# Two transformer blocks on one core: copies of short rows, compressed turns, column sums and the first weight unit rearranged

## What is computed

```python
def first_block(x, ...):
    h = rms_norm(x, attn_pre_norm)
    mix = hybrid_mixer(h, ...)            # differential attention (4 heads) and sparse attention (8 heads)
    x = x + rms_norm(mix, attn_post_norm)
    h = rms_norm(x, ffn_pre_norm)
    return x + rms_norm((silu(h @ w_gate) * (h @ w_up)) @ w_down, ffn_post_norm)

# in hybrid_mixer: proj = h @ w_in gives dq, dk, dv, nq, kc, vc, ks, vs, kw, vw, gates
# differential: a = softmax(q1 k1) - lam * softmax(q2 k2), causal;  o = a @ v;  rms_norm per head
# sparse: o = g0 * o_cmp + g1 * o_slc + g2 * o_win  (compressed tokens, selected blocks, window)
```

## Time and profile before

| | |
|---|---|
| median of 3 runs | 1940.08 us (1939.52 to 1940.37) |
| the profiled execution | 1938.64 us, its span 1936.7 us |
| TensorE matmul | 1889.7 us busy, 98% |
| TensorE weight load | 1525.7 us, 79% |
| VectorE | 823.8 us, 43% |
| ScalarE | 427.4 us, 22% |
| GpSimd | 1231.2 us, 64% |

### The profile page before, as it was taken

The page is one execution under the profiler, slowest core; times in us unless marked ns, Lnnn a source line. Parts: engine busy times, 40 slices in busy tenths (PEclk is TensorE's granted clock), DMA queues, the critical chain, the costliest instruction groups (busy, mean ns, idle before and its releaser), DMA issues.

```text
span 1936.7 us, 25810 instructions
## 1 busy us (share of the span) xinstructions
PE 1889.7 (98%) x9462; PEld 1525.7 (79%) x9462; DVE 823.8 (43%) x1419; ACT 427.4 (22%) x868; POOL 1231.2 (64%) x737
## 2 busy tenths in 40 slices
PE   9999989999999999999999999999999999999997
PEld 7876558888888888866888888889877888888886
DVE  6345872633432025424453434104993464334103
ACT  4333651311110012015221111002333331111000
POOL 7973544866666558654786667656757586666662
PEclk9999999999999999999999999999999999999998
DMA  6431002233333224330233333221323222333311
GB/s 205 132 119 44 1 2 72 76 92 97 90 111 105 90 62 141 88 98 2 76 98 97 91 93 123 93 81 52 109 76 98 77 84 90 97 93 111 105 60 44
DMA packets 44879, 168.30 MB, mean 87 GB/s; under 512 B 4984, under 2 KB 7288, under 8 KB 44672
## 3 DMA queue, kind: packets, MB, share of 16 engines
q1 hardware_dynamic: 44064, 162.99, 27.5%
q10 hardware_dynamic: 736, 4.21, 0.5%
HBM read 165.07 MB, written 2.11 MB: 86 GB/s over the span
## 4 chain that ended last, share of the span: by engine, by line
PE 81%; DVE 6%; POOL 3%; issue 2%; ACT 1%; POOLq 0%; DVEq 0%; ACTq 0%
PE psum L496 25%; PE psum L498 25%; PE psum L497 25%; POOL w_lo L408 1%; DVE h_lo L1351 1%; PE psum L676 1%; DVE tmp L1393 1%; PE psum L690 1%; PE psum L541 1%; DVE e_ring L1508 1%; POOL w_hi L405 1%; POOL x L419 1%; PE psum L717 0%; PE psum L549 0%; PE psum L763 0%
## 5 line engine op out<-in xcount | busy, mean ns | idle before, releaser
L408 POOL TENSOR_TENSOR w_lo<-raw,w_hi 128x1024 fp32r<-128x1024 f32 (+1 forms) x287 | 753.0, 2624 | 23.9
L496 PE MATMUL psum<-h_hi,w_hi 128*128 128x512 f32 (+1 forms) x1816 | 689.8, 380 | 10.8 <-POOL w_lo L408 6.8
L497 PE MATMUL psum<-h_lo,w_hi 128*128 128x512 f32 (+1 forms) x1816 | 685.4, 377 | 0.0
L498 PE MATMUL psum<-h_hi,w_lo 128*128 128x512 f32 (+1 forms) x1816 | 685.3, 377 | 0.0
L405 POOL TENSOR_SCALAR w_hi<-raw 128x1024 fp32r<-128x1024 f32 (+1 forms) x287 | 325.0, 1132 | 514.0 <-PE psum L498 484.0
L496 PEld LDWEIGHTS psum<-h_hi,w_hi 128*128 128x128 f32 x1816 | 342.1, 188 | 83.3 <-issue 10.3
L498 PEld LDWEIGHTS psum<-h_hi,w_lo 128*128 128x128 f32 x1816 | 341.9, 188 | 70.3
L497 PEld LDWEIGHTS psum<-h_lo,w_hi 128*128 128x128 f32 x1816 | 341.9, 188 | 69.3 <-issue 0.2
L496 PE MATMUL psum<-g_hi,w_hi 128*128 128x512 f32 (+1 forms) x594 | 219.9, 370 | 0.0
L497 PE MATMUL psum<-g_lo,w_hi 128*128 128x512 f32 (+1 forms) x594 | 219.4, 369 | 0.0
L498 PE MATMUL psum<-g_hi,w_lo 128*128 128x512 f32 (+1 forms) x594 | 219.3, 369 | 0.0
(11 more groups left out here) (261 smaller groups left out, 1797.5 us busy)
## 6 DMA issues: line engine op xcount, KB each, us to landing
raw<-in_wide SPq DMA_DIRECT2D x239, 512.0 KB, 3.6
raw<-in_down SPq DMA_DIRECT2D x48, 704.0 KB, 4.0
x<-in_xt ACTq DMA_DIRECT2D x4, 512.0 KB, 6.8
decay<-decay_rows ACTq DMA_DIRECT2D x1, 2048.0 KB, 7.5
out<-x SPq DMA_DIRECT2D x16, 128.0 KB, 1.7
o_diff<-in_angles SPq DMA_DIRECT2D x1, 512.0 KB, 6.8
cols<-in_cols SPq DMA_DIRECT2D x1, 221.0 KB, 4.0
tabs<-in_tables SPq DMA_DIRECT2D x1, 208.0 KB, 6.0
```

The source lines that it names most:

```text
L408: nc.gpsimd.tensor_tensor(w_lo[:, slot, 0:w], raw[:, j % RAW, 0:w], w_hi[:, slot, 0:w].bitcast(F32), ALU.subtract).then_inc(units_split, 1)
L496: pe.matmul(out_ap, lhs[0], rhs[0], start=first, stop=False)
L497: pe.matmul(out_ap, lhs[0], rhs[1], start=False, stop=False)
L498: return pe.matmul(out_ap, lhs[1], rhs[0], start=False, stop=last)
```

## The change

Five edits. (1) Copies of the transposed maps: ScalarE makes one in every step, and in sparse steps with i of 0 or 1 it copies both banks; VectorE only bank 5 of sparse steps with i of 2 or 3. The one-instruction combination stays on VectorE for i = 3 alone; i = 2 goes to GpSimd as a product and a sum. (2) `cmp_turn` 1 and 2 with their scores stand behind dv1 and dv2. (3) The last square of an opening norm goes to PSUM, VectorE adds it to `total` too, and `col_stat` makes one column sum; it stands behind chunk 2 of the fourth unit, `row_stat` behind chunk 5. (4) Opening: unit 0 is split in halves (`split_first`); SyncE loads x's last three quarters right behind unit 0 and no longer waits; TensorE takes the first four chunks of kc when the first half is split, and from the fourth on alternates chunks of kc and vc, three apart; the column sum stands behind vg0 and the row behind vg1. (5) ScalarE loads its first table ahead of x, and takes lambda's exponential ahead of the squares.

```diff
-BOTH_BY_DVE = (0, 1)
+COPIED_BY_ACT = (0, 1)
 def combined_by_dve(t):
-    return STEPS[t][0] == "diff" and STEPS[t][3] >= 2
+    return STEPS[t][0] == "diff" and STEPS[t][3] == NB - 1
 def copies_by_dve(upto):
-    return sum(step[0] == "nsa" or step[3] in BOTH_BY_DVE for step in STEPS[:upto])
+    return sum(step[0] == "nsa" and step[3] not in COPIED_BY_ACT for step in STEPS[:upto])
...
                 for j in range(peel):
-                    if j == 1:
-                        sp.wait_ge(x_landed[2], 16)
                     load(tiles, source, j, j)
+                    for q in range(1, 4 if j == 0 else 0):
+                        sp.dma_start(x[:, 2 * q:2 * q + 2, :], xt[:, 2 * q:2 * q + 2, :]).then_inc(x_landed[q], 16)
...
+            def split_first(tiles):
+                w = tiles * P
+                pool.wait_ge(weights_landed[0], n.take("landed_0", 16))
+                pool.sem_inc(unit_taken, 1)
+                for part, high_done, low_done in ((slice(0, w // 2), first_high, first_half), (slice(w // 2, w), high_split, units_split)):
+                    nc.gpsimd.tensor_scalar(w_hi[:, 0, part], raw[:, 0, part], 1.0, 1.0, ALU.mult, ALU.mult).then_inc(high_done, 1)
+                    pool.wait_ge(high_done, 1)
+                    nc.gpsimd.tensor_tensor(w_lo[:, 0, part], raw[:, 0, part], w_hi[:, 0, part].bitcast(F32), ALU.subtract).then_inc(low_done, 1)
+                n.take("units")
...
             def col_stat():
-                pe.wait_ge(summed, n.take("summed", SUMS))
-                add_columns(total, True, False)
-                pe.wait_ge(squared, n.take("squared", KC))
-                add_columns(squares[:, (KC - 1) % 2, :], False, True)
+                n.take("squared", KC)
+                pe.wait_ge(summed, n.take("summed", KC - 1))
+                add_columns(total, True, True)
...
-                    if t == 0:
+                    if t == 2:
                         col_stat()
-                    if t == 3:
+                    if t == 5:
                         row_stat()
...
-            feature("kc", 0)
-            feature("vc")
-            pe.wait_ge(summed, n.take("summed", KC - 1))
-            n.take("squared", KC)
-            add_columns(total, True, True)
+            n.take("units_split", 2)
+            for t in range(KC + 3):
+                for u, c in ((0, t), (1, t - 3)):
+                    if not 0 <= c < KC:
+                        continue
+                    if u == 0:
+                        pe.wait_ge(h_low, c + 1)
+                    if c in (0, KC // 2):
+                        pe.wait_ge(units_split if u or c else first_half, u + 1)
+                    mm = three(psum[:, u, :], [w_hi[:, u, c * P:(c + 1) * P], w_lo[:, u, c * P:(c + 1) * P]], h_of(c), c == 0, c == KC - 1)
+                    if c == KC - 1:
+                        mm.then_inc(unit_done, 1)
             pe.wait_ge(lam_exped, 1)
-            for u in token_units("vg", (3, 3, 2), VG, row_stat):
-                pass
+            for u in token_units("vg", (3, 3, 2), VG):
+                if u == 0:
+                    col_stat()
+                if u == 1:
+                    row_stat()
...
             for u in token_units("dv", (2, 2, 2, 2), 4 * P):
-                if u in (0, 1):
-                    cmp_turn(u + 1)
-                    cmp_scores(u + 2)
+                if u in (1, 2):
+                    cmp_turn(u)
+                    cmp_scores(u + 1)
...
-                place = total[:] if j == 0 else squares[:, 1, :] if j == KC - 1 else psum[:, 4 + j % 2, :]
+                place = psum[:, 4 + j % 2, :] if j else total[:]
...
-                    if 0 <= r < len(STEPS) and STEPS[r][3] not in BOTH_BY_DVE:
+                    if 0 <= r < len(STEPS):
...
-                        copy(t_ring[:, r % 2, 0, 0:w], psum[:, 4 + (r % 2 if STEPS[r][0] == "diff" else 0), 0:w]).then_inc(pair_copied_act, 1)
+                        if STEPS[r][0] == "nsa" and STEPS[r][3] in COPIED_BY_ACT:
+                            copy(t_ring[:, r % 2, :, 0:w], psum[:, 4:6, 0:w]).then_inc(pair_copied_act, 1)
+                        else:
+                            copy(t_ring[:, r % 2, 0, 0:w], psum[:, 4 + (r % 2 if STEPS[r][0] == "diff" else 0), 0:w]).then_inc(pair_copied_act, 1)
...
-            for j in range(4):
-                act.dma_start(x[:, 2 * j:2 * j + 2, :], xt[:, 2 * j:2 * j + 2, :]).then_inc(x_landed[j], 16)
+            act.dma_start(x[:, 0:2, :], xt[:, 0:2, :]).then_inc(x_landed[0], 16)
+            act.wait_ge(set_up, 1)
+            copy(spare[:], ones[:, 0:1])
...
-                    n.take("squared")
+                    add_square(KC - 1)
```

More of the change, by code:

```diff
@@ L143, in combined_by_dve @@
 def combined_by_dve(t):
-    return STEPS[t][0] == "diff" and STEPS[t][3] >= 2
-def copies_by_act(upto):
-    return sum(step[3] not in BOTH_BY_DVE for step in STEPS[:upto])
+    return STEPS[t][0] == "diff" and STEPS[t][3] == NB - 1
 def copies_by_dve(upto):
-    return sum(step[0] == "nsa" or step[3] in BOTH_BY_DVE for step in STEPS[:upto])
+    return sum(step[0] == "nsa" and step[3] not in COPIED_BY_ACT for step in STEPS[:upto])
 FOX_STEPS = [(c, i) for c in range(4) for i in reversed(range(NB))]
@@ L280, in two_blocks @@
             sem(s) for s in ("cols_landed", "tabs_landed", "decay_stored", "decay_landed", "stored"))
-        unit_taken, high_split, units_split = sem("unit_taken"), sem("high_split"), sem("units_split")
+        unit_taken, high_split, units_split, first_high, first_half = (
+            sem(s) for s in ("unit_taken", "high_split", "units_split", "first_high", "first_half"))
         x_ready, x_final, half_done = sem("x_ready"), sem("x_final"), sem("half_done")
@@ L474, in _ @@
                 for j in range(peel):
-                    split(tiles, j)
+                    if j == 0:
+                        split_first(tiles)
+                    else:
+                        split(tiles, j)
                 times, rest = divmod(count - peel, SLOTS)
@@ L660, in copied @@
             def copied(upto):
-                pe.wait_ge(pair_copied_act, copies_by_act(upto))
+                pe.wait_ge(pair_copied_act, upto)
                 pe.wait_ge(pair_copied_dve, copies_by_dve(upto))
@@ L788, in free_bank, with token_units @@
                 return A_BANK[name]
-            def token_units(name, tiles_of_unit, width, after_first=lambda: None, first_bank=None):
+            def token_units(name, tiles_of_unit, width, first_bank=None):
                 k = 0
@@ L1042, in norm @@
                         square(c - 1, x[:, c - 1, :])
-                n.take("summed", SUMS)
+                n.take("summed", KC - 1)
                 roots()
@@ L1121, in _ @@
                 copy(h_hi[:, c, :], x[:, c, :], scale=col("attn_pre", c)).then_inc(h_high, 1)
+            act.wait_ge(lam_summed, 1)
+            nc.scalar.activation(lam[:, 2:4], psum[:, 4, 0:2], ACT.Exp).then_inc(lam_exped, 1)
             for c in range(KC):
@@ L1336, in root_and_spread, with stat @@
                 dve.wait_ge(row_spread, n.take("row_spread"))
-            def stat(columns=2):
+            def stat(columns=1):
                 dve.wait_ge(column_added, n.take("column_added", columns))
@@ L1528, in pair_attention @@
                     r = t - PAIR_TURN
-                    if 0 <= r < len(STEPS) and (STEPS[r][0] == "nsa" or STEPS[r][3] in BOTH_BY_DVE):
-                        kind, i = STEPS[r][0], STEPS[r][3]
-                        w = (i + 1) * P
+                    if 0 <= r < len(STEPS) and STEPS[r][0] == "nsa" and STEPS[r][3] not in COPIED_BY_ACT:
+                        w = (STEPS[r][3] + 1) * P
                         dve.wait_ge(pair_transposed, r + 1)
@@ L1534, in pair_attention @@
                             dve.wait_ge(pair_mixed, r - 1)
-                        if kind == "diff":
-                            v.tensor_copy(t_ring[:, r % 2, 0, 0:w], psum[:, 4 + r % 2, 0:w]).then_inc(pair_copied_dve, 1)
-                        elif i in BOTH_BY_DVE:
-                            v.tensor_copy(t_ring[:, r % 2, :, 0:w], psum[:, 4:6, 0:w]).then_inc(pair_copied_dve, 1)
-                        else:
-                            v.tensor_copy(t_ring[:, r % 2, 1, 0:w], psum[:, 5, 0:w]).then_inc(pair_copied_dve, 1)
+                        v.tensor_copy(t_ring[:, r % 2, 1, 0:w], psum[:, 5, 0:w]).then_inc(pair_copied_dve, 1)
                     r = t - PAIR_MIX - 1
@@ L1607, in _ @@
             v.tensor_scalar(lam[:, 5:6], lam[:, 4:5], -LAM_INIT, None, ALU.add).then_inc(set_up, 1)
-            stat(1)
+            stat()
             for j in range(2):
```

4 lines of the change are left out of this document (removed).

## The result

The changed kernel takes **1920.53 us** (median of 4 runs, 1919.96 to 1921.54) against 1940.22 us of the kernel before (4 runs, 1939.52 to 1943.39): a ratio of 0.9896, 95% interval 0.9879 to 0.9913. The forecast was 1922.4. The profiled execution took 1920.00 us with a span of 1918.2, 18.6 under the span before. In a later comparison on another occasion the ratio was 0.9896 again (0.9882 to 0.9910; 1921.06 and 1941.14 us).

The account below looks back on a forecast made before the run. TensorE, busy for 98% of the span, was taken as the bound, with its waits and lower clock. Opening +3.1, turns -8.6, attention -9.2 and norms -3.0 sum to -17.7 us, giving 1922.4 us, range 1913 to 1932.

Parts of the forecast that it names:

- Rival 1: TensorE's low-clock dips move to other places in attention, opening and norms instead of going; 1929.9 us, chance 0.13.
- rivals 2: Attention: copies only change engine, TensorE waits as long as before, gain 0; 1931.6 us, chance 0.12.
- 4 (slower): Attention loop has no slack, so moved copies and GpSimd pairs lie fully on the path; 1951 us, chance 0.02.
- Rival 3: Halves work and norms hide row sums: opening -0.5, norms -4.5, attention -12; 1914.5 us, chance 0.07.
- Turns, -8.6: Compressed turns: with turn 1 behind dv1, its 4.25 us wait and the low clock go; -8.6 us (-7.5 to -9).
- Sparse steps, -4.6 and -3.1: First attention's 32 later steps: -4.6 us from fewer copy waits, -3.1 us from the dip at 250 going.
- First 16 steps, -1.5: First attention's first 16 steps: copy waits go, GpSimd's i=2 pair returns part; -1.5 us (bounds -4 and 0).
- 4 x 0.4: First 16 steps: of 1.05 us of waits a head, 0.65 returns for GpSimd, leaving 0.4 in four heads.
- 194.83: First 16 steps: time in us when TensorE wants the i=2 row, 195.88 less 1.05 of a head's waits.
- Opening norms, -3.0: Five norms: halved column sums give -4.2 us, fifth unit's 0.3 us waits in four cost 1.2; -3.0 (-1.5 to -4.5).
- three dips: Low-clock stretches behind TensorE waits: 2.5 us in the opening, 4.25 at the compressed turn, 1.8 in the first attention.
- Opening, +3.1: Opening: kc and vc end 1.35 us later, new wait of 1.8 before nq0; +3.1 us (-0.5 to +5).

Follow-up runs that it names:

- e1_turns: Kernel before with only compressed turns 1 and 2 and their scores moved behind dv1 and dv2; 1932.75 us, ratio 0.9963.
- e3_norms: Kernel before with only the opening norms' edit (one column sum behind chunk 2, row behind chunk 5, last square added by VectorE); 1934.20 us, ratio 0.9970.
- e2_attention: Kernel before with only the attention's edits (copies on ScalarE, i = 2 pair on GpSimd); 1934.89 us, ratio 0.9975.
- e5_pair_back: Changed kernel with the i = 2 combination of the differential steps back on VectorE as one instruction; 1915.34 us, ratio 0.9875.
- e9_changed_again: The changed kernel run once more, unaltered, as the measure for other kernels; 1921.06 us, ratio 0.9896.
- e10_best: Changed kernel with i = 2 back on VectorE, kc six chunks ahead of vc, vc placed first, norms' row sum behind chunk 4; 1908.80 us, ratio 0.9838.
- e4_opening: Kernel before with only the opening's edits; 1940.82 us against 1940.75, ratio 0.9999.
- e11_row_at_4: Changed kernel with the opening norms' row sum behind chunk 4 of the fourth unit instead of 5; 1917.66 us, ratio 0.9882.

## Why the prediction was right, step by step

**The total.** Forecast -17.7 on the span, measured -18.6; the medians stand 19.7 apart in the first comparison and 20.1 in the last. Part of that closeness is luck: the first 16 steps gave 1.3 us less than forecast and the norms 1.5 us more. The parts do add: alone they give -8.0, -5.9, -6.5 and +0.1 us by the medians, -20.3 together. Rival 1 (dips move) falls with e1_turns to e3_norms, rivals 2 (copies only change engine) and 4 (slower) with e2_attention. Rival 3 was right for the norms, and for the attention as soon as the pair goes back.

**Turns, -8.6.** Measured -8.7, alone and together. That the wait of 4.25 us and the low level behind it go together holds in 14 profiles: a low stretch near 145 in all six with turn 1 behind dv0, none in the other eight. The same goes for the dip near 250: in all six with VectorE's two-bank copies, in none of the eight with ScalarE's.

**Sparse steps, -4.6 and -3.1.** Measured -7.6. Waits in this stage fell by 4.6 us, from 7.6 (7.1 for the two-bank copies, 0.5 for one of bank 5) to 3.0: the rows for L451 and L1555 above, less one wait of 0.70 at 203.87, which lies ahead of the stage's first mark. About 2.8 are the low stretch. The forecast left 1.7 us of waits with GpSimd and at the heads' ends and 1.2 with VectorE; 2.1 and 0.8 are there.

**First 16 steps, -1.5.** Measured -0.2. The price of the pair was right (2.3 taken; 1.24 + 1.00 and a gap of 0.08). The step that failed is "4 x 0.4", a gain of 0.4 us in each of four heads. TensorE's transposes of the first two i = 2 rows show it, in the kernel before, the changed one and e5_pair_back:

```profile
179.06 0.55 PE L690 MATMUL psum<-tabs,e_ring 128*128 128x128 f32 x3
187.47 0.55 PE L690 MATMUL psum<-tabs,e_ring 128*128 128x128 f32 x3
```

```profile
173.78 0.55 PE L699 MATMUL psum<-tabs,e_ring 128*128 128x128 f32 x3 [0.91 <-POOL e_ring L448]
181.88 0.55 PE L699 MATMUL psum<-tabs,e_ring 128*128 128x128 f32 x3 [1.15 <-POOL e_ring L448]
```

```profile
172.75 0.55 PE L699 MATMUL psum<-tabs,e_ring 128*128 128x128 f32 x3
179.63 0.55 PE L699 MATMUL psum<-tabs,e_ring 128*128 128x128 f32 x3
```

The six waits of 3.2 us stand between 184.15 and 202.84, two in each of three heads, and the sum took them for four. Ahead of the first i = 2 row no wait for a copy goes, so the new wait of 0.91 is a plain loss there: from turn 3 to this row it is 9.38 us before, 10.37 in the changed kernel and 9.39 in e5_pair_back. That is 1.0 us lost where 0.4 was to be won, as much as the whole error. In the other three heads the gain was near the forecast, 0.3 us a head (8.41 to 8.10 from one such row to the next), though both of its terms were too small. Without the pair a head takes 6.88 us: the copies gave 1.53 and not 1.05, so TensorE wants the row 0.48 us earlier than the 194.83 of the prediction (taken from the third head), and waits 1.15 us for it and not 0.65. e5_pair_back shows that there was no need to give GpSimd that row. By the rule of the Trainium skill (SBUF — State Buffer, section Who interferes with whom) as the prediction read it, the term would have been near zero. That is its size, but the trace shows another cause: VectorE's coefficient for the first such row was ready at 171.29, and at 171.24 in e5_pair_back, ahead of the pair; the next one, beside the pair, took 0.22 us, as without it. It was the pair itself that was late.

**Opening norms, -3.0.** Measured -4.4 to -4.5, of which 3.2 are work. The fifth unit's wait was put at 0.3 us in four norms and is 0.19 in three and 0.87 in one. What was missing is the low stretch behind the two sums. The prediction counts three dips and overlooks the fourth, at 363, and it has a dip at a norm only as a possible loss (rival 1), not as something that the edit removes; in other runs of the kernel before there are more of them, and these, with the longer form of the old opening, are the known parts of what the medians show beyond the traces.

**Opening, +3.1.** Measured +2.5 against before's profile. The mechanism came as forecast: split of the first half done at 9.0 (8.7), unit 1 whole at 15.94 (15.9), kc and vc at 26.0, and at 27.3 in e9_changed_again (27.1), 1.9 us before nq0 (1.8). Two sizes were off. Unit 0's split begins at 6.73, 0.9 us earlier than before and not 1.5; unit 1 is whole at the forecast time only because the splits of both units took 9.2 us and not 9.7, which is luck. As the prediction read the Trainium skill's rule (DMA: Bandwidth & Descriptors, section Issuing engines are not separate DMA queues), unit 0 would have landed when it did before. It came earlier: the split begins at 6.7 to 7.1 in the eight profiles in which x's last three quarters stand behind unit 0, and at 7.7 to 8.1 in the six in which they stand beside it. That this order is the cause, and no other edit of the opening, wasn't tried apart. And TensorE's first product came at 10.40 and not 9.2, as its 14 warming products ran longer at the low level (9.11 us against 7.82 before); in e9_changed_again and e10_best they didn't. The later start did not cost anything: in the three profiles of this opening with the first product at 10.4 to 10.5 the low level lasts 3.4 us and kc and vc end at 26.0 to 26.1, in the three with it at 9.2 to 9.5 it lasts 6.8 us and they end at 26.9 to 27.3. Which of the two comes is not set by the kernel, so that 27.1 came true in one kind of execution only. The larger error is one that a single profile hid: I took 56.6 us as the length of the old opening, which in five profiles is 56.6 to 60.7, 58.6 on average. The changed one is 59.0 to 60.3 in five (the changed kernel twice, e4_opening, e5_pair_back, e11_row_at_4), 59.7 on average. And the low level in the old opening, which the prediction counts as 2.8 us lost, was hidden behind the h_lo chunks (kc and vc end at 25.8 with it and at 25.9 without). So the term is nearer +1, and e4_opening measures 0 with an uncertainty of 2 us.

## What to carry to other kernels

Price a wait with what stands behind it: of the 20.9 us that turns, attention and norms gave, about 8.4 were clock (8.7 less the wait of 4.25 at the turn, 2.8 in the sparse steps by 79.1 and 77.7 us at two lengths of the dip, 1.2 at the norm). A work item moved off an engine must fit in front of the time at which its consumer will come after the change, not before it; put it back and measure that first. And look at several executions of the kernel before where two engines take turns: an opening can have two forms, and a load that comes later can choose the better one.

## What the runs showed of the hardware

The low level came behind waits much shorter than the 1.8 us that I looked for: behind a wait of 0.7 to 1.0 us and, one chunk later, 1.7 us of column sums, in 9 of 25 norms; with the same sums two chunks further behind the wait, in none of five (one profile). The wait of 1.9 us before nq0, with full units before and behind it, was followed by none in any of the six kernels that have it. The rise of the clock after the kernel's start differs by 3.0 us between executions (4.1 us in e4_opening, 7.1 in e3_norms): 3 to 6 of the 13 distances between warming products are 0.85 us or more, one lies between, the others are 0.43. Their code is the same everywhere, and in two executions of the changed kernel the rise came at 6.8 and 5.0.
